# RMS norms of xa_q and ffn_up moved behind the matmul, with epilogues by half groups

## The chip, the cores and the metric

The kernel runs on one core of a Trainium2 chip. The metric is its device time in microseconds (us). Lower is better.

## The reference

One call computes two transformer blocks on 256 tokens of width 2048, batch 1. The second block ends with these steps (RMS norm, cross attention and a convolved, gated feed-forward part):

```python
def rmsnorm(x, w):
    y = xf * lax.rsqrt(jnp.mean(xf * xf, axis=-1, keepdims=True) + NORM_EPS)
    return (y * w)

h = h + merged @ w_mix_out[l]
hn = rmsnorm(h, norm_xa_w[l])
mem_n = rmsnorm(mem, norm_mem_w[l])
h = h + memory_cross_attention(hn, mem_n, xa_w_q[l], xa_w_k[l], xa_w_v[l], xa_w_o[l])
hn = rmsnorm(h, norm_ffn_w[l])
h = h + conv_gated_ffn(hn, ffn_w_up[l], ffn_conv_w[l], ffn_conv_b[l], ffn_w_down[l])
return rmsnorm(h, final_norm_w)
```

The attention has 4 heads of 512 over 256 memory tokens. The feed-forward part multiplies by a weight of 2048 x 11264, runs a causal convolution with three taps over the tokens, takes silu of one half times the other half, and multiplies by a weight of 5632 x 2048. The factor rsqrt(mean) is one number per token, and the weight is one number per feature.

## The kernel before, in words

**Data.** Activations lie with features on the 128 partitions and tokens along the row: x is 16 chunks of 128 features, each of 256 tokens. Every operand of a matmul is split into a high and a low part of type fp32r ("pair"): ScalarE copies the high part, VectorE subtracts it from the value and writes the low part. a_pair and b_pair are two such activations of 16 chunks.

**Units.** The weights stream from memory in units of 128 x 1024 (512 KB). A ring of four slots holds raw, w_hi and w_lo. For each unit SP loads raw (L572), ScalarE casts w_hi (L1154), VectorE subtracts w_lo (L1717), and PE multiplies. A unit is four chunks of the input for 256 output features. Per chunk there are two matmuls of w_hi with high and low tokens (512 columns, L688) and two of w_lo with the high tokens (256 columns, L692). The high and low products lie side by side in the accumulator.

**Stages.** `STAGES` lists the matrices in order; the four engines walk through it with loops of their own and meet through counting semaphores. In mode "F" a group of units gives two chunks of output (256 features); with 16 chunks of input a group is 4 units, and groups alternate between two halves of the accumulator. A stage of 2048 x 2048 has 32 units. ffn_up has 11 iterations of 16 units (two groups of gate features, two of value features), ffn_down has 88 units. Between stages nothing stops the stream of units: `unit_at` lets the walk of a stage split the first four units of the next one.

**The order on ScalarE and VectorE** is written out in `walk`. When unit j ends a group, they do, in this order: the join (ScalarE copies the low product to halves_b, L1185; VectorE adds it to the high product into buf_a, L1784); the split of unit j + 4; after every second group the first part of the stage's epilogue ("whole"), on four chunks; and after the split of unit j + 5 the epilogue's rest. A `side` function runs at given units j, ahead of the split. The last stage's end has no following unit, so the rest runs at once.

**Epilogues around the change.** mix_out and xa_o: VectorE adds buf_a to x (L2222), ScalarE squares (L1490), VectorE reduces the squares of four chunks to one (L2232). After the last unit PE sums over the partitions with a matrix of ones (`sums_of`, L719). Then come ScalarE's root (`rms`, L1247), VectorE's reciprocal (L1822), and `pair`: eight times two chunks of x times weight times rstd (L1849), high part (L1262), low part (L1831). `pair_ready` counts them, and the next stage's PE waits for two counts per unit. ffn_up: after two groups ScalarE does four Identities with bias and scale (L1654), VectorE eight convolution steps (L2569). For the gate half ScalarE then applies silu (L1662). For the value half VectorE multiplies with the gate (L2576), ScalarE copies the high part (L1664) and VectorE subtracts the low part of h_pair (L2581).

**Attention** runs as a side function in xa_q and xa_o: at units 9, 10 and 11 after the start of each head's eight units PE computes scores (L1052), transposes (L1061) and the product with the values (L1072). The scores wait for `dve_done`, which VectorE raises once the head's four chunks of xa_qf are written. Its keys and values (mem_k, mem_v, 2 MB each) are loaded by SP ahead of xa_q's units (L604, L605).

Of the kernel before, what the change touches and what calls it, by code (L numbers as in the profile page):

```python
# [94 lines left out]
class Stage:  # L95
    def __init__(self, name, weights, mode, iters, group_units=DC // KU, groups=2, ada=None, gate=False, act=1, dve=0, ready=0):
        self.name, self.weights, self.mode, self.iters = name, weights, mode, iters
# [116 lines left out]
for _place, _n in MOD_PLACE.items():  # L214
# [10 lines left out]
    ("rglru", 16, 36, 16), ("xa_norm", 1, 1, 0), ("xa_pair", 0, 8, 8), ("attention", 12, 12, 8),  # L225
    ("ffn_norm", 1, 1, 0), ("ffn_pair", 0, 8, 8), ("final", 1, 1, 1),
# [36 lines left out]
def rg_root_step(q):  # L263
# [5 lines left out]
            xa=68, xa_o=72, ffn=80, ffn_down=91)  # L269

# [65 lines left out]
def build(nc, t):  # L336

    ctx = ExitStack()
    with ctx:
# [14 lines left out]
        w_lo = sb("w_lo", [P, RING, KU, NCOL], F32R)  # L354
        a_pair = sb("a_pair", [P, 2, DC, T], F32R)
        a_hi, a_lo = Half(a_pair, 0), Half(a_pair, 1)
        x = sb("x", [P, DC, T])
# [60 lines left out]
        xa_qf = wk("xa_qf", [P, DC, T], 32 * K)  # L418
        xa_kf = wk("xa_kf", [P, DC, T], 48 * K)
        xa_vt = wk("xa_vt", [P, 2, D], 64 * K)  # L420
# [3 lines left out]
        h_pair = wk("h_pair", [P, 2, FC, T], 0, F32R)  # L424
# [15 lines left out]
        mean = sb("mean", [P, T])  # L440

# [61 lines left out]

        def used(stage):

            return RING + stage.u0 + stage.total
# [8 lines left out]
        def _(sp):  # L515
# [39 lines left out]
            def load(stage):  # L555
                for i in rounds(sp, stage.iters):
                    for j, (kind, g, k, _) in enumerate(stage.kinds):
# [3 lines left out]
                        if stage.name == "merge_a" and j == 2 * RING:  # L561

                            sp.wait_ge(unit_used, used(STAGE["ret_proj"]))
                            nc.sync.dma_start(rg_w[:], t["rg_w"]).then_inc(rg_in, 16)

                        sp.wait_ge(lo_done, i * stage.n + (u + 1))
                        if kind == "w":
                            src, at_ = t[stage.weights], i * stage.n_w + (g * stage.group_units + k)
                        else:
                            src, at_ = t["w_gate"], k  # L570
# [4 lines left out]
            for stage in STAGES:  # L575
# [23 lines left out]
                if stage.name == "xa_q":  # L599

                    sp.wait_ge(pair_ready, PAIR["mix_out"])
                    sp.wait_ge(kv_stored[0], 16 * 5)
                    sp.wait_ge(kv_stored[1], 16 * 5)
                    nc.sync.dma_start(flat(xa_kf), t["mem_k"]).then_inc(xa_in, 16)  # L604
                    nc.sync.dma_start(flat(xa_vt), t["mem_v"]).then_inc(xa_in, 16)  # L605
# [11 lines left out]
        def _(pe):  # L617
# [94 lines left out]
            def sums_of(stage, with_mean=False):  # L712

                for q in range(4):

                    pe.wait_ge(dve_done, DVE_DONE[stage] - 2 * (3 - q))
# [316 lines left out]
            sums_of("mix_out")  # L1033
            steps.end("xa_norm")
            steps.end("xa_pair")


# [45 lines left out]
            steps.end("ffn_norm")  # L1083
            steps.end("ffn_pair")


            run("ffn_up", a_pair, PAIR["xa_o"], batch=2)
# [54 lines left out]
        def _(act):  # L1142
# [24 lines left out]
            def run(name, group, side=None):  # L1167
# [8 lines left out]
                def finish(i, g, n_used):  # L1176
# [14 lines left out]
                    return whole if g % 2 and group else None  # L1191
# [52 lines left out]
            def rms(name):  # L1244

                steps.wait(pe=1)
                steps.done(nc.scalar.activation(spare[:], msc[:, 0, 0:T], ACT.Sqrt, bias=tiny[:, 21:22],  # L1247
# [365 lines left out]
            run("mix_out", with_squares(None))  # L1613
            rms("xa_norm")
            pair(a_hi, "xa_pair")


            def attention(first):

                def side(j):  # L1620
# [13 lines left out]
                    if step == 2:  # L1634

                        steps.wait(pe=3 * h + 3)
                        steps.done(nc.scalar.copy(b_hi[:, 4 * h:4 * h + 4, :].rearrange("p a b -> p (a b)"),
# [5 lines left out]
            run("xa_q", with_dve(None), side=attention(0))  # L1643
            run("xa_o", with_squares(None), side=attention(STAGE["xa_q"].n))
            rms("ffn_norm")
            pair(a_hi, "ffn_pair")


            def gate_and_value(i, g):
                dst = buf_b if g == 0 else buf_c  # L1650

                for m in range(4):
                    at_ = FC * g + m
# [4 lines left out]
                def rest():  # L1658

                    act.wait_ge(dve_done, dve.add())  # L1660
                    if g == 0:
                        ran(nc.scalar.activation(flat(buf_b), flat(buf_b), ACT.Silu))  # L1662
                    else:
                        ran(nc.scalar.copy(flat(h_hi)[:, bass.ds(i * (4 * T), 4 * T)], flat(buf_c)))  # L1664
                return rest

            run("ffn_up", gate_and_value)
# [37 lines left out]
        def _(dve):  # L1705
# [59 lines left out]
            def run(name, group, between=None, side=None, dest=None):  # L1765
# [4 lines left out]
                def finish(i, g, n_used):  # L1770
# [15 lines left out]
                    def whole():  # L1786
                        dve.drain()
                        return group(i, g // 2)
                    return whole if g % 2 else None
# [29 lines left out]
            def reciprocal_of_root(n):  # L1819
# [3 lines left out]
                dve.drain()  # L1823

# [694 lines left out]
            run("mix_out", residual(1.0))  # L2519
            reciprocal_of_root(1)  # L2520
            steps.end("xa_norm")
            pair(a_hi, a_lo, rms_of(x, "norm_xa"), "xa_pair")


            def attention(first):

                def side(j):
# [14 lines left out]
                    if step == 2:  # L2542

                        steps.wait(act=3 * h + 3)
                        vec.tensor_tensor(b_lo[:, 4 * h:4 * h + 4, :].rearrange("p a b -> p (a b)"),  # L2545
                                          msc[:, 2:4, :].rearrange("p a b -> p (a b)"),
                                          b_hi[:, 4 * h:4 * h + 4, :].bitcast(F32).rearrange("p a b -> p (a b)"),
# [5 lines left out]
            run("xa_q", finished, side=attention(0), dest=in_slab(xa_qf))  # L2553
            run("xa_o", residual(1.0), side=attention(STAGE["xa_q"].n))
            reciprocal_of_root(1)
            steps.end("ffn_norm")
            pair(a_hi, a_lo, rms_of(x, "norm_ffn"), "ffn_pair")


            def gate_and_value(i, g):  # L2560
                wait_act()
                dst = buf_b if g == 0 else buf_c

                for shift in (1, 2):
                    if shift == 2:
                        dve.drain()
                    for m in range(4):
                        weight = prm[:, bass.ds(i * 4 + (COL["ffn_conv_w"] + 2 * FC * (2 - shift) + FC * g + m), 1)]
                        vec.scalar_tensor_tensor(dst[:, m, shift:T], buf_a[:, m, 0:T - shift], weight,  # L2569
                                                 dst[:, m, shift:T], ALU.mult, ALU.add)  # L2570
                dve.drain()
                if g == 0:
# [3 lines left out]
                ran(vec.tensor_tensor(flat(buf_c), flat(buf_c), flat(buf_b), ALU.mult))  # L2576

                def rest():

                    wait_act()  # L2580
                    vec.tensor_tensor(flat(h_lo)[:, bass.ds(i * (4 * T), 4 * T)], flat(buf_c),  # L2581
                                      flat(h_hi)[:, bass.ds(i * (4 * T), 4 * T)].bitcast(F32),
                                      ALU.subtract).then_inc(pair_ready, 1)
                return rest

            run("ffn_up", gate_and_value)
# [152 lines left out]
```

## Time and profile before

| what | value |
|---|---|
| median of 3 runs | 3309.81 us (3309.08 to 3312.45) |
| profiled execution, its own time | 3308.2 us |
| its span, first to last instruction | 3306.4 us |
| mean granted TensorE clock | 0.973 |
| PE busy | 3120.8 us, 94% |
| PE weight loads busy | 2679.6 us, 81% |
| VectorE (DVE) busy | 2213.5 us, 67% |
| ScalarE (ACT) busy | 1626.0 us, 49% |
| GpSimd (POOL) busy | 55.6 us, 2% |
| chain that ended last | PE 84%, DVE 9%, ACT 3% |
| memory traffic | 662.04 MB, mean 200 GB/s |

The profile is one execution. Busy times of the engines overlap. In its rows L688 is line 688 of the kernel, "out<-in" are the kernel's names. PE's granted clock is given as a share of full speed, 2.4 GHz. The profiled execution's own time is its span and 1.8 us around it.

### The profile page before, as it was taken

Reading aid. Unit: us, or ns where it says so; the run is one execution under the profiler, and the core shown is the slowest. Engines: PE = TensorE matmul, PEld = TensorE weight load, DVE = VectorE, ACT = ScalarE, POOL = GpSimd, SP = SyncE. Lnnn points to the kernel's source line nnn. Section 1 sums busy time; section 2 is a strip of 40 time slices with the busy share of each in tenths; the row PEclk is TensorE's granted clock in tenths of the full one; section 3 lists DMA queues with packets and bytes.
Section 4 is the critical chain, followed back from the end, with each engine's and each line's share of the span. In section 5 each row is a group of like instructions: output and inputs, shape, how many; then the busy total and the mean of one; then the engine's idle time right before and its main releaser. Section 6 shows DMA issues by size and latency. Waiting matters only on the chain.

```text
span 3306.4 us, 45891 instructions
## 1 busy us (share of the span) xinstructions
PE 3120.8 (94%) x16880; PEld 2679.6 (81%) x16880; DVE 2213.5 (67%) x2661; ACT 1626.0 (49%) x1886; POOL 55.6 (2%) x52
## 2 busy tenths in 40 slices
PE   7999898999979997899999989998998999999997
PEld 5878787788868886688888878887887888888886
DVE  7667877668867877755665785566546667766444
ACT  5555444245544455543454665444434566655432
POOL 0000330000000000000000000000000000000000
PEclk9999999999989998899999999999999999999999
DMA  7887667377737764464455545556444555555553
GB/s 279 320 311 252 226 218 258 118 270 281 273 125 235 278 235 146 135 193 144 153 197 190 174 158 187 188 189 218 134 145 146 186 193 188 181 195 186 191 188 127
DMA packets 179516, 662.04 MB, mean 200 GB/s; under 512 B 20004, under 2 KB 20388, under 8 KB 178216
## 3 DMA queue, kind: packets, MB, share of 16 engines
q1 hardware_dynamic: 177704, 655.89, 58.7%
q10 hardware_dynamic: 1664, 4.19, 0.3%
q8 instruction: 91, 1.49, 0.2%
q14 instruction: 57, 0.47, 0.0%
HBM read 653.71 MB, written 6.29 MB: 200 GB/s over the span
## 4 chain that ended last, share of the span: by engine, by line
PE 84%; DVE 9%; ACT 3%; DVEq 2%; issue 2%; DMA 1%; ACTq 0%; SPq 0%
PE acc L688 44%; PE acc L692 22%; PE acc L699 4%; PE acc L701 4%; PE acc L700 4%; DVE w_lo L1717 2%; ACT w_hi L1154 1%; DVE gate_ratio L2472 1%; PE msc L646 1%; PE msc L648 1%; DVE mod_raw L1728 1%; DMA mod_raw<-in_w_mod 1%; PE msc L798 0%; PE acc L850 0%; PE msc L1052 0%
## 5 line engine op out<-in xcount | busy, mean ns | idle before, releaser
L1717 DVE TENSOR_TENSOR w_lo<-raw,w_hi 128x1024 fp32r<-128x1024 f32 x1020 | 1242.5, 1227 | 713.2 <-ACT w_hi L1154 704.4
L688 PE MATMUL acc<-a_pair,w_hi 128*128 128x512 f32 x4864 | 1546.8, 399 | 47.1 <-DVE w_lo L1717 16.0
L1154 ACT CAST w_hi<-raw 128x1024 fp32r<-128x1024 f32 x1020 | 1062.7, 1049 | 914.4 <-PE acc L692 679.5
L692 PEld LDWEIGHTS acc<-a_pair,w_lo 128*128 128x128 f32 x4864 | 919.8, 189 | 218.0
L692 PE MATMUL acc<-a_pair,w_lo 128*128 128x256 f32 x4864 | 960.5, 279 | 0.0
L688 PEld LDWEIGHTS acc<-a_pair,w_hi 128*128 128x128 f32 x4864 | 750.6, 190 | 56.9 <-issue 34.9
L688 PE MATMUL acc<-b_pair,w_hi 128*128 128x512 f32 x1280 | 402.3, 396 | 2.4 <-DVE b_pair L2545 2.4
L692 PEld LDWEIGHTS acc<-b_pair,w_lo 128*128 128x128 f32 x1280 | 240.4, 188 | 56.8
L699 PE MATMUL acc<-w_hi,a_pair 128*128 128x512 f32 x640 | 255.1, 399 | 27.4 <-DVE w_lo L1717 16.2
L1185 ACT COPY halves_b<-acc 128x512 f32<-128x512 f32 x200 | 117.3, 586 | 314.0 <-PE acc L692 313.9
L700 PE MATMUL acc<-w_hi,a_pair 128*128 128x512 f32 x640 | 253.4, 396 | 0.0
L701 PE MATMUL acc<-w_lo,a_pair 128*128 128x512 f32 x640 | 253.1, 396 | 0.0
L692 PE MATMUL acc<-b_pair,w_lo 128*128 128x256 f32 x1280 | 251.4, 278 | 0.0
L688 PE MATMUL acc<-h_pair,w_hi 128*128 128x512 f32 x704 | 221.2, 395 | 0.7 <-DVE w_lo L1717 0.7
L688 PEld LDWEIGHTS acc<-b_pair,w_hi 128*128 128x128 f32 x1280 | 194.9, 189 | 2.8 <-DVE b_pair L2545 2.8
L1784 DVE TENSOR_TENSOR buf_a<-acc,halves_b 128x512 f32<-128x512 f32 x160 | 110.7, 692 | 124.5 <-ACT halves_b L1185 118.5
L699 PEld LDWEIGHTS acc<-w_hi,a_pair 128*128 128x128 f32 x640 | 122.9, 192 | 55.6 <-DVE w_lo L1717 18.0
L1728 DVE SCALAR_TENSOR_TENSOR mod_raw<-mod_raw,cond_wide 128x1024 f32<-128x1024 f32 x128 | 160.0, 1250 | 10.1 <-DMA mod_raw<-in_w_mod 6.7
L692 PEld LDWEIGHTS acc<-h_pair,w_lo 128*128 128x128 f32 x704 | 132.2, 188 | 31.3
L701 PEld LDWEIGHTS acc<-w_lo,a_pair 128*128 128x128 f32 x640 | 122.7, 192 | 26.3
L700 PEld LDWEIGHTS acc<-w_hi,a_pair 128*128 128x128 f32 x640 | 122.9, 192 | 25.5
L692 PE MATMUL acc<-h_pair,w_lo 128*128 128x256 f32 x704 | 138.3, 278 | 0.0
(319 smaller groups left out, 1974.3 us busy)
## 6 DMA issues: line engine op xcount, KB each, us to landing
raw<-in_w_ffn_up SPq DMA_DIRECT2D x176, 512.0 KB, 4.2
mod_raw<-in_w_mod SPq DMA_DIRECT2D x128, 512.0 KB, 5.2
raw<-in_w_ffn_down SPq DMA_DIRECT2D x88, 512.0 KB, 3.7
ada_raw<-in_w_ada SPq DMA_DIRECT2D x64, 512.0 KB, 5.5
raw<-in_w_xa_k SPq DMA_DIRECT2D x32, 512.0 KB, 5.1
raw<-in_w_xa_v SPq DMA_DIRECT2D x32, 512.0 KB, 4.6
raw<-in_w_k SPq DMA_DIRECT2D x32, 512.0 KB, 4.3
raw<-in_w_v SPq DMA_DIRECT2D x32, 512.0 KB, 5.1
```

Of the source, the lines that this page charges most:

```text
L646: pe.matmul(msc[:, bank, :], cond_pair[:, kc, :], w_hi[:, slot, c, :], start=(first and c == 0), stop=False)
L648: mm = pe.matmul(msc[:, bank, :], cond_pair[:, kc, :], w_lo[:, slot, c, :], start=False, stop=(last and c == KU - 1))
L688: pe.matmul(acc[:, 2 * (g % 2) + m, :], w_h[:, cols], pair[:, :, kc, :], start=begin, stop=False, skip_group_check=True)
L692: mm = pe.matmul(acc[:, 2 * (g % 2) + m, 0:T], w_l[:, cols], pair[:, 0, kc, :], start=False, stop=end, skip_group_check=True)
L699: pe.matmul(out, xh, w_hi[:, slot, c, :], start=begin, stop=False)
L700: pe.matmul(out, xl, w_hi[:, slot, c, :], start=False, stop=False)
L701: mm = pe.matmul(out, xh, w_lo[:, slot, c, :], start=False, stop=end)
L1154: nc.scalar.copy(w_hi[:, slot], source).then_inc(hi_done, 1)
L1185: nc.scalar.copy(halves_b[:], low_part(g)).then_inc(part_copied, 1)
L1717: vec.tensor_tensor(w_lo[:, slot], source, w_hi[:, slot].bitcast(F32), ALU.subtract).then_inc(lo_done, 1)
L1728: vec.scalar_tensor_tensor(mod_raw[:, n % MOD_RING], mod_raw[:, n % MOD_RING], 1.0, cond_wide[:, half * (D // 2):(half + 1) * (D // 2)], A ...
L1784: vec.tensor_tensor(out, main_part(g), halves_b[:], ALU.add).then_inc(acc_free, 1)
```

## The change

- mix_out and xa_o run their epilogue after every half group (two chunks, one group of units) instead of every four chunks. VectorE adds to x. ScalarE writes the high part of x times the norm's weight (without the token factor), VectorE the low part, which raises `pair_ready`. After every second half group come square and reduce, as before. mix_out becomes one iteration of eight half groups instead of two of four.
- The token factor is computed in a side function at unit 3 (`NORM_AT`) of the following stage: PE's sums, ScalarE's root, VectorE's reciprocal. `xa_norm` and `ffn_norm` keep their steps, `xa_pair` and `ffn_pair` are gone.
- xa_q and ffn_up multiply each half group's result by the token factor on VectorE, after the split of unit j + 4.
- ffn_up is divided into ffn_first (one iteration, 16 units) and ffn_up (10 iterations), and its epilogue runs on two chunks after each group of units.
- The load of mem_k and mem_v stands at unit 10 of mix_out. Buffers are placed anew: xa_q reads b_pair, xa_o reads a_pair, ffn_up reads a new f_pair, h_pair begins where a_pair lies.

```diff
-    Stage("mix_out", "w_mix_out", "F", 2, act=1, dve=2),
+    Stage("mix_out", "w_mix_out", "F", 1, groups=4, act=3, dve=3),
     Stage("xa_q", "w_xa_q", "F", 1, groups=4, act=0, dve=1),
-    Stage("xa_o", "w_xa_o", "F", 1, groups=4, act=1, dve=2),
-    Stage("ffn_up", "w_ffn_up", "F", 11, act=2, dve=1, ready=0.5),
+    Stage("xa_o", "w_xa_o", "F", 1, groups=4, act=3, dve=3),
+    Stage("ffn_first", "w_ffn_up", "F", 1, act=4, dve=4, ready=0.5),
+    Stage("ffn_up", "w_ffn_up", "F", 10, act=4, dve=4, ready=0.5, first_unit=2 * DC // KU),
...
+NORM_AT = 3
...
+                        if stage.name == "mix_out" and j == 10:
+
+                            sp.wait_ge(dve_done, DVE_DONE["rnn_proj"])
+                            sp.wait_ge(kv_stored[0], 16 * 5)
+                            sp.wait_ge(kv_stored[1], 16 * 5)
+                            nc.sync.dma_start(flat(xa_kf), t["mem_k"]).then_inc(xa_in, 16)
+                            nc.sync.dma_start(flat(xa_vt), t["mem_v"]).then_inc(xa_in, 16)
...
-                if stage.name == "xa_q":
-
-                    sp.wait_ge(pair_ready, PAIR["mix_out"])
...
             run("mix_out", a_pair, PAIR["rnn_proj"], batch=4)
-            sums_of("mix_out")
-            steps.end("xa_norm")
-            steps.end("xa_pair")
+            def token_sums(stage, name):
+
+                def side(j):
+                    if j == NORM_AT:
+                        sums_of(stage)
+                        steps.end(name)
+                return side
...
-            run("xa_q", a_pair, PAIR["mix_out"], batch=2, side=attention(0))
-            run("xa_o", b_pair, PAIR["xa"], batch=4, side=attention(STAGE["xa_q"].n))
-            sums_of("xa_o")
...
-            run("ffn_up", a_pair, PAIR["xa_o"], batch=2)
+            run("xa_q", b_pair, PAIR["mix_out"], batch=2, side=both_sides(token_sums("mix_out", "xa_norm"), attention(0)))
+            run("xa_o", a_pair, PAIR["xa"], batch=4, side=attention(STAGE["xa_q"].n))
+            run("ffn_first", f_pair, PAIR["xa_o"], batch=2, side=token_sums("xa_o", "ffn_norm"))
+            run("ffn_up", f_pair, PAIR["ffn"])
             run("ffn_down", h_pair, PAIR["ffn"], batch=4)
...
+            def scaled_and_squares(hi, weight):
+                def group(i, g):
+                    def rest():
+                        act.wait_ge(dve_done, dve.add())
+                        for c in range(2 * g, 2 * g + 2):
+                            mm = nc.scalar.activation(hi[:, c, :], x[:, c, :], ACT.Copy, scale=col(weight, c))
+                        ran(mm)
+                        if g % 2:
+                            ran(nc.scalar.activation(both, flat(x)[:, (g - 1) * (2 * T):(g + 1) * (2 * T)], ACT.Square))
...
                     def whole():
                         dve.drain()
-                        return group(i, g // 2)
-                    return whole if g % 2 else None
+                        if scale:
+
+                            mm = vec.tensor_tensor(out, out, bcast(scale, 2), ALU.mult)
+                            if g % 2 or by_half:
+                                ran(mm)
+                        if by_half:
+                            return group(i, g)
+                        return group(i, g // 2) if g % 2 else None
+                    return whole if g % 2 or scale or by_half else None
...
+            def residual_and_low(hi, lo, weight):
+                def group(i, g):
+                    part = flat(x)[:, g * (2 * T):(g + 1) * (2 * T)]
+                    ran(vec.tensor_tensor(part, part, flat(buf_a)[:, g % 2 * (2 * T):(g % 2 + 1) * (2 * T)], ALU.add))
+                    def rest():
+                        dve.drain()
+                        wait_act()
+                        for c in range(2 * g, 2 * g + 2):
+                            mm = vec.scalar_tensor_tensor(lo[:, c, :], x[:, c, :], col(weight, c), hi[:, c, :].bitcast(F32),
+                                                          ALU.mult, ALU.subtract)
+                        mm.then_inc(pair_ready, 1)
+                        if g % 2:
+                            wait_act()
+                            ran(vec.tensor_reduce(buf_b[:, g // 2, :], buf_a[:].rearrange("p c t -> p t c"), AX, ALU.add))
...
-                    for m in range(4):
+                    for m in range(2 * half, 2 * half + 2):
...
-                ran(vec.tensor_tensor(flat(buf_c), flat(buf_c), flat(buf_b), ALU.mult))
+                ran(vec.tensor_tensor(flat(buf_c)[:, part], flat(buf_c)[:, part], flat(buf_b)[:, part], ALU.mult))
```

## Rows read from the trace of the kernel before

**Rows 1.** Windows: length, busy us (instructions) of PE, PEld, DVE, ACT, POOL, clock, DMA.

```profile
2748.40:2793.00 44.60, 44.60 (x257) 38.90 (x256) 31.04 (x38) 26.74 (x32) 0.00 (x0) 1.00 0.58 188
...
2299.15:2314.52 15.37, 2.52 (x9) 1.32 (x8) 11.04 (x15) 6.20 (x8) 0.00 (x0) 0.66 0.35 115
...
2530.21:2545.39 15.18, 2.51 (x9) 1.29 (x8) 10.77 (x14) 6.20 (x8) 0.00 (x0) 0.70 0.21 69
```

**Rows 2.** PE's waits after 2280 us: waiter, releaser, us, times, longest.

```profile
PE msc L719 <- DVE buf_b L2232: 16.7, 3, 6.3
...
PE msc L1052 <- DVEq L1814: 0.9, 4, 0.3
...
PE acc L688 <- DVE w_lo L1717: 0.7, 1, 0.7
```

**Rows 3.** Timeline, mix_out to xa_q: start, length, engine, operation, [idle before <- releaser].

```profile
2298.75 0.40 PE L692 MATMUL acc<-a_pair,w_lo 128*128 128x256 f32 x2
...
2298.99 1.46 PE L719 MATMUL msc<-buf_b,ones 128*128 128x256 f32 x6
2299.26 0.59 ACT L1185 COPY halves_b<-acc 128x512 f32<-128x512 f32 x1 [0.97 <-PE acc L692]
...
2302.23 1.23 DVE L2222 SCALAR_TENSOR_TENSOR x<-x,buf_a 128x1024 f32 x1 [0.18 <-issue]
2303.59 1.06 ACT L1490 ACTIVATE buf_a<-x 128x1024 f32 x1 [2.80 <-DVE x L2222]
...
2304.78 1.89 DVE L2232 TENSOR_REDUCE buf_b<-buf_a 128x1024 f32 x1 [1.32 <-ACT buf_a L1490]
...
2308.49 1.75 DVE L1822 RECIPROCAL rstd<-spare 128x256 f32<-128x256 f32 x1 [1.82 <-ACT spare L1247]
...
2313.73 0.68 DVE L1831 TENSOR_TENSOR a_pair<-buf_a,a_pair 128x512 fp32r<-128x512 f32 x1
...
2314.52 1.19 PE L688 MATMUL acc<-a_pair,w_hi 128*128 128x512 f32 x2 [6.57 <-issue]
```

**Rows 4.** Timeline, xa_o to ffn_up: PE's last and first matmuls.

```profile
2529.81 0.39 PE L692 MATMUL acc<-b_pair,w_lo 128*128 128x256 f32 x2
...
2545.39 1.22 PE L688 MATMUL acc<-a_pair,w_hi 128*128 128x512 f32 x2 [6.70 <-DVE a_pair L1831]
```

**Rows 5.** Timeline, the first head's scores in xa_q.

```profile
2340.19 1.22 DVE L1717 TENSOR_TENSOR w_lo<-raw,w_hi 128x1024 fp32r<-128x1024 f32 x1 [0.26 <-ACT w_hi L1154]
...
2340.97 0.39 PE L692 MATMUL acc<-a_pair,w_lo 128*128 128x256 f32 x2
...
2341.66 3.69 PE L1052 MATMUL msc<-xa_kf,xa_qf 128*128 128x256 f32 x16 [0.29 <-DVEq L1814]
```

**Rows 6.** Timeline of ACT and of DVE in one iteration of ffn_up.

```profile
2748.47 0.59 ACT L1185 COPY halves_b<-acc 128x512 f32<-128x512 f32 x1 [1.81 <-PE acc L692]
...
2749.96 2.08 ACT L1654 ACTIVATE buf_b<-buf_a,prm 128x256 f32<-128x256 f32 x4
...
2770.77 0.59 ACT L1185 COPY halves_b<-acc 128x512 f32<-128x512 f32 x1 [1.81 <-PE acc L692]
...
2774.48 1.67 DVE L2569 SCALAR_TENSOR_TENSOR buf_c<-buf_a,prm,buf_c 128x255 f32<-128x255 f32 x4 [0.91 <-ACT buf_c L1654]
...
2779.20 1.22 DVE L1717 TENSOR_TENSOR w_lo<-raw,w_hi 128x1024 fp32r<-128x1024 f32 x1
...
2782.85 2.36 DVE L1717 TENSOR_TENSOR w_lo<-raw,w_hi 128x1024 fp32r<-128x1024 f32 x2 [0.98 <-ACT w_hi L1154]
```

**Rows 7.** Timeline, start of ffn_down.

```profile
3048.72 3.49 DVE L1717 TENSOR_TENSOR w_lo<-raw,w_hi 128x1024 fp32r<-128x1024 f32 x3
...
3049.99 0.74 PE L688 MATMUL acc<-h_pair,w_hi 128*128 128x512 f32 x2 [0.67 <-DVE w_lo L1717]
```

**Rows 8.** Timeline, the first splits of xa_q behind the load of mem_k and mem_v.

```profile
2294.68 1.05 ACT L1154 CAST w_hi<-raw 128x1024 fp32r<-128x1024 f32 x1 [5.11 <-DMA raw<-in_w_xa_q]
...
2295.76 3.79 DVE L1717 TENSOR_TENSOR w_lo<-raw,w_hi 128x1024 fp32r<-128x1024 f32 x3 [4.93 <-ACT w_hi L1154]
```

More of the change, by code:

```diff
@@ L1242, in with_dve, with rms @@
                 return wrapped
-            def rms(name):
+            def rms(name, root=spare):
                 steps.wait(pe=1)
-                steps.done(nc.scalar.activation(spare[:], msc[:, 0, 0:T], ACT.Sqrt, bias=tiny[:, 21:22],
+                steps.done(nc.scalar.activation(root[:], msc[:, 0, 0:T], ACT.Sqrt, bias=tiny[:, 21:22],
                                                 scale=1.0 / D))
@@ L1641, in attention, with gate_and_value @@
                 return side
[L1643 to L1650, printed above, removed]
-                for m in range(4):
-                    at_ = FC * g + m
+            run("xa_q", with_dve(None), side=both_sides(token_root("xa_norm"), attention(0)))
+            run("xa_o", scaled_and_squares(f_hi, "norm_ffn"), side=attention(STAGE["xa_q"].n), by_half=True)
+            def gate_and_value(first, i, g):
+                half = g % 2
+                dst = buf_b if g < 2 else buf_c
+                act.wait_ge(dve_done, dve.add())
+                for m in range(2 * half, 2 * half + 2):
+                    at_ = FC * (g // 2) + 4 * first + m
                     mm = nc.scalar.activation(dst[:, m, :], buf_a[:, m, :], ACT.Identity, bias=prm[:, bass.ds(i * 4 + (COL["ffn_conv_b"] + at_), 1)],
@@ L1660, in rest @@
                     act.wait_ge(dve_done, dve.add())
[L1661 to L1662 removed]
+                    part = flat(dst)[:, half * (2 * T):(half + 1) * (2 * T)]
+                    if g < 2:
+                        ran(nc.scalar.activation(part, part, ACT.Silu))
                     else:
[L1664 removed]
+                        ran(nc.scalar.copy(flat(h_hi)[:, bass.ds(i * (4 * T) + (first * (4 * T) + half * (2 * T)), 2 * T)], part))
                 return rest
[L1667 removed]
+            run("ffn_first", lambda i, g: gate_and_value(0, i, g), side=token_root("ffn_norm"), by_half=True)
+            run("ffn_up", lambda i, g: gate_and_value(1, i, g), by_half=True)
             run("ffn_down", with_squares(None))
@@ L1763, in make_gates, with run @@
                 steps.done(vec.reciprocal(gate_tmp[64:P, 3, :], gate_tmp[64:P, 1, :]))
-            def run(name, group, between=None, side=None, dest=None):
+            def run(name, group, between=None, side=None, dest=None, scale=None, by_half=False):
                 stage = STAGE[name]
@@ L1823, in reciprocal_of_root, with token_reciprocal, side @@
                 dve.drain()
+            def token_reciprocal(name):
+                def side(j):
+                    if j == NORM_AT:
+                        steps.wait(act=1)
+                        vec.reciprocal(token_scale[:], token_scale[:])
+                        dve.drain()
+                        steps.end(name)
+                return side
             def pair(hi, lo, make, name, before=None):
@@ L2518, in _ @@
             run("rnn_proj", merge_second)
[L2519 to L2522, printed above, removed]
+            def residual_and_low(hi, lo, weight):
[3 more added lines that the diff above has]
+                    def rest():
+                        dve.drain()
+                        wait_act()
[6 more added lines that the diff above has]
+                            ran(vec.tensor_reduce(buf_b[:, g // 2, :], buf_a[:].rearrange("p c t -> p t c"), AX, ALU.add))
+                    return rest
+                return group
+            run("mix_out", residual_and_low(b_hi, b_lo, "norm_xa"), by_half=True)
             def attention(first):
@@ L2551, in attention, with gate_and_value @@
                 return side
[L2553 to L2560, printed above, removed]
+            run("xa_q", lambda i, g: None, side=both_sides(token_reciprocal("xa_norm"), attention(0)), dest=in_slab(xa_qf),
+                scale=token_scale)
+            run("xa_o", residual_and_low(f_hi, f_lo, "norm_ffn"), side=attention(STAGE["xa_q"].n), by_half=True)
+            def gate_and_value(first, i, g):
+                half = g % 2
                 wait_act()
-                dst = buf_b if g == 0 else buf_c
+                dst = buf_b if g < 2 else buf_c
                 for shift in (1, 2):
```

84 lines of the change are left out of this document (50 added, 34 removed).

## The prediction

> **What bounds the kernel now.** I read the page first: PE is busy for 3120.8 of 3306.4 us, and the chain that ended last is 84% PE. So time can only be won where PE stands still or runs slowly. Next I read the windows, stage by stage. In ffn_up PE is busy for all 44.60 us of one iteration at a granted clock of 1.00, with VectorE at 31.04 and ScalarE at 26.74 us [rows 1]. Between mix_out and xa_q, and again between xa_o and ffn_up, are stretches of 15.37 and 15.18 us with 2.5 us of PE work each and a clock of 0.66 and 0.70 [rows 1]. Third, PE's waits over the last 1000 us: besides those two places there is little, 0.9 us in four waits before the attention scores and 0.7 us at the start of ffn_down [rows 2].
>
> The timeline of the first boundary shows the ladder [rows 3]. PE's last matmul ends at 2299.15. Then follow, one after the other, a w_lo split, x (1.23 us), the square (1.06), the reduce (1.89), the last column sum, root, reciprocal and the first scaled chunks. PE starts xa_q at 2314.52. The second boundary is alike: 2530.2 to 2545.39 [rows 4].
>
> **What the two boundaries cost today.** A unit (four chunks) takes PE (2770.77 - 2748.47) / 8 = 2.7875 us at full clock [rows 6]. After the first gap nine units end at 2341.37, 26.85 us after the start instead of 25.09 [rows 3, 5]: 1.76 us, since the clock was still at 1.2 instead of 2.4 GHz for the first chunks. After the second, the group that ScalarE picks up at 2748.47 ended at 2748.36 (0.11 before, as at 2299.26 against 2299.15 [rows 3, 6]). That is 202.97 us after 2545.39, instead of 72 units or 200.70: 2.27 us. Together 15.37 + 1.76 + 15.18 + 2.27 = **34.58 us**.
>
> **The change, part by part.**
>
> *Norm moved behind the matmul.* xa_q and ffn_up now multiply the unscaled x times the norm's weight, so their first units need neither root nor reciprocal. xa_q's unit k reads the 4(k+1)-th chunk at most, and each half group of mix_out signals two chunks. Units 0 to 2 need half groups 0 to 5, which ended more than two unit lengths before. Unit 3 needs half group 7. PE can therefore go from mix_out's last unit straight into units 0 to 2, which last 8.36 us. The two other conditions hold too: accumulators alternate, and the four slots of weights ahead are filled as before.
>
> Now the last half group, counted from PE's end (0 = 2299.15) [rows 3]: the w_lo split before x is over at 2.90, x starts at 3.08 and takes 0.69 on 512 columns (like a_pair's 0.68) to 3.77; two scaled copies on ScalarE, 0.49 us apart and 0.6 long (buf_b's four take 2.08 [rows 6]), to 4.95; low halves, two of about 0.45, to 5.9; square to 6.1; reduce of 1.89 to 8.1. Unit 3's chunks are ready 2.5 us early, and the last column sum is ready 0.3 us before PE asks for it at 8.36. So the gap and the slow start both go: -34.58.
>
> *What PE now pays.* The eight matmuls of the sums stand in the stream before unit 3. Six took 1.46 us [rows 3], so eight cost 1.95, twice: **+3.9**. Root and reciprocal (the latter 1.75 us [rows 3]) must be over before VectorE scales the group that ends with unit 3, at 8.36 + 1.95 + 2.79 = 13.1. They are: sums end at 10.3, reciprocal by about 13.4 behind a w_lo, and the scale multiply comes only after another w_lo. The first weight split of the new stage that queues behind the reduce ends at about 9.3 and is due at 13.1.
>
> *Scale multiply in xa_q.* One more VectorE instruction of 128x512 after each half group, behind the w_lo. For each of the four heads PE already waits for exactly that point: w_lo ends at 2341.41, the scores start at 2341.66 [rows 5], and PE was free at 2341.37. The multiply replaces a drain and adds about 0.7 us to each head: **+2.8**. A multiply with a broadcast operand isn't in the trace; from below it is a plain one (0.68), from above two of them (1.37), which would add another 2.8. I take 0.69, as its sizes are those of the plain row.
>
> *ffn_up by half groups.* On VectorE each iteration gains four multiplies (2.76 us) and splits two operations of 1024 columns. Two of 0.685 for one of 1.23 is 0.14 more each. 31.04 + 2.76 + 0.29 = 34.1 of 44.6 us: it is covered on average. The local deadline matters more. Slots allow w_lo of the unit five further on to end four units (11.15 us) after the group's end, and the next one at 13.94. Today, from the value group's end (2770.66), they end at 9.76 and 13.4 [rows 6]: only 0.5 us to spare on the second, because four Identities, eight convolution steps, a 1024-wide product and a table load stand in one heap. New: w_lo 2.9, multiply to 3.8, two Identities to 4.95, four convolution steps of 0.42 with their drain to 7.0 (today eight in 3.5 [rows 6]), half product to 7.7, w_lo to **8.95**. ScalarE's cast of the half to 8.5, table load to 9.8, next cast, and w_lo to 12.2. Both are earlier than today, so I cost the whole edit at nothing. If the cover went, each microsecond past 11.15 would be paid in each of 44 half groups.
>
> A rule of the Trainium skill speaks against just this. *VectorE: DVE Perf Modes*, section "The TRN2 errata — SBUF-src ops pay a fixed extra latency per instruction", says that many small tiles pay a fixed latency each, and advises 512 elements or more. Its fp32 formula (N + 151) / 0.96 gives 0.69 us for 512 columns; the trace agrees (0.68 to 0.69). By it a split costs 0.157 us instead of the rows' 0.14: for 22 splits 3.5 against 3.1 us of VectorE. The sum would be 3.5 or 3.1 worse only if VectorE were the bound there.
>
> *Start of ffn_down.* PE waited 0.67 us for a w_lo that starts at 3048.72, right behind the low half of h [rows 7]. The half-wide ladder is some 3 us shorter (two Identities, four steps, and half of product, cast and low half less, the multiply more): **-0.7**. The same ladder now stands between ffn_first and the loop; by it w_lo ends some 0.6 us before its deadline.
>
> *The load of mem_k and mem_v* moves from before xa_q's units into mix_out, at unit 10. Today it holds the next cast until 2294.68, and three w_lo run to 2299.55, the first to 2297.0, before PE needs it at 2299.15 [rows 8]: 2 us to spare. The waits in front of it (rnn_proj done) are met long before; SP keeps the same order of two large transfers and then a unit. In mid-stage the same delay meets the same slack: nothing. If PE came to wait it would be 1 to 4 us, once.
>
> *Extra work in mix_out and xa_o*: per pair of half groups four scaled copies (2 us) on ScalarE, and four low halves (1.8) and 0.15 on VectorE, in 22.3 us that hold eight splits of 1.23, two joins, x and a reduce, together 14.4. Covered.
>
> Sum: -34.58 + 3.9 + 2.8 - 0.7 = **-28.6 us**. The profiled execution took 3308.2 (span 3306.4 and 1.8 around it), so 3279.6. The median shown, 3309.81, is 1.6 above that execution; carried over: **3281.3**.
>
> **Rivals.**
> A: the half-group ladder becomes the bound in ffn_up, so the kernel is slower. Place: ScalarE and VectorE hand over four times per half group, now 44 times instead of 22. For it: only 0.5 us to spare today [rows 6] and multiplies added. Against: 8.95 against 11.15. It outweighs the gain from 28.6 / 44 = 0.65 us of stall each, that is, a ladder 2.85 us longer than worked out. At 0.8 us: 35.2 - 28.6 = +6.6, 3316.4.
> B: the same ladder slips a little, at loop boundaries where the table load stands: 0.3 to 0.8 us in each of 11 iterations, 3285 to 3290.
> C: the last sum isn't ready. The margin is 0.3 us, the ladder has four handovers, and scaled copies of this form with Copy are not in the trace. 1 us late at both places: 3283. For it the small margin, against it that every duration has a near row.
> D: the burst in mix_out stalls PE: +1 to 4, 3282 to 3285.
> E: the change doesn't do what it says, PE still waits for the last pair before unit 0: the gap shrinks only by root, reciprocal and sum (about 5 us each), 3300. Against: the counts above.
>
> **Chances.** Forecast 0.77 (own range 3278 to 3285), A 0.03, B 0.08, C 0.05, D 0.04, E 0.02; another 0.01 for no change. Unknown prices reach from the attention's multiplies hidden (-2.8) to a double-priced broadcast (+2.8) and sums at 0.38 instead of 0.24 us a matmul (+2.2). The range 3277 to 3288 takes these in and most of B, C and D. About 0.2% (6.6 us) is what a measurement of this kernel can tell from no change: faster 0.95, same 0.02, slower 0.03.
>
> **What would show it.** PE's waits after 2200 us hold no entry of 6 us; the granted clock stays 1.00 across both boundaries; eight sum matmuls of about 1.95 us stand between units 2 and 3. The waits before the scores grow from 0.9 to about 3.7 us in four. In ffn_up PE is busy throughout and VectorE's share rises to about 76%. ffn_down starts without a wait. I would be wrong if PE shows waits for w_lo in ffn_up, or a wait at the sums above 0.5 us.

## The result, and the profile after

| | before | after |
|---|---|---|
| median | 3309.44 us (3308.07 to 3312.45, 4 runs) | 3283.93 us (3279.66 to 3287.07, 4 runs) |
| ratio | | 0.9922 (95% interval 0.9906 to 0.9938) |
| profiled execution, its span | 3308.2, 3306.4 us | 3283.0, 3281.2 us |
| granted clock | 0.973 | 0.976 |

The kernel is 25.5 us faster, 0.8%, where the prediction's sum was 28.6; 3283.93 lies inside the range of 3277 to 3288.

The windows of the changed kernel over both boundaries and one iteration of ffn_up (length, then busy us and instructions of PE, PEld, DVE, ACT, POOL, then granted clock, DMA share, GB/s) answer to [rows 1]:

```profile
2299.00:2330.00 31.00, 30.64 (x175) 26.60 (x173) 21.02 (x21) 15.63 (x19) 0.00 (x0) 1.00 0.55 177
...
2519.00:2545.00 26.00, 26.00 (x149) 22.69 (x148) 19.63 (x21) 16.11 (x20) 0.00 (x0) 1.00 0.49 162
...
2719.50:2764.10 44.60, 44.60 (x257) 38.90 (x256) 34.22 (x45) 24.44 (x32) 0.00 (x0) 1.00 0.56 188
```

Both gaps are gone and the clock stays at full speed across them. VectorE's share in ffn_up rose from 31.04 to 34.22 us, PE is busy throughout.

PE's waits after 2150 us (waiter, releaser, us in total, times, longest) answer to [rows 2]:

```profile
PE msc L735 <- DVE buf_b L2292: 4.5, 1, 4.5
PE msc L1072 <- DVE xa_qf L1833: 3.6, 4, 1.0
PE acc L704 <- DVE a_pair L2623: 2.4, 1, 2.4
PE acc L704 <- DVE w_lo L1760: 1.6, 1, 1.6
PE msc L1081 <- DVE prob L2618: 0.8, 4, 0.2
```

The first is the end of the kernel and was there before, as were the third and the fifth. The scores' wait grew from 0.9 to 3.6 us. The fourth is new. The wait at the start of ffn_down [rows 7] is gone.

The timeline of the first boundary, all engines (start, length, engine, operation, [idle before <- releaser]), answers to [rows 3]:

```profile
2303.36 1.05 ACT L1172 CAST w_hi<-raw 128x1024 fp32r<-128x1024 f32 x1
...
2305.76 0.69 DVE L2584 TENSOR_TENSOR x<-x,buf_a 128x512 f32<-128x512 f32 x1
...
2306.55 0.91 ACT L1641 ACTIVATE b_pair<-x,prm 128x256 fp32r<-128x256 f32 x2 [2.14 <-DVE x L2584]
...
2307.49 0.88 DVE L2591 SCALAR_TENSOR_TENSOR b_pair<-x,prm,b_pair 128x256 fp32r<-128x256 f32 x2 [1.04 <-ACT b_pair L1641]
...
2308.44 2.05 DVE L2597 TENSOR_REDUCE buf_b<-buf_a 128x256 f32<-128x1024 f32 x1
...
2311.03 1.89 PE L735 MATMUL msc<-buf_b,ones 128*128 128x256 f32 x8
```

ScalarE picked up mix_out's last group at 2302.87, so PE ended it at 2302.76 and went straight on. Until the sums it ran three units of xa_q. The reduce was over at 2310.5, 7.7 us after that end (forecast: 8.1).

**Where the time went.** ScalarE's copy of each group's low product (0.11 us after PE's last matmul of the group) is a mark in both traces:

| stretch | before | after | difference |
|---|---|---|---|
| start to the end of rnn_proj's last group but one (same code) | 2209.78 | 2211.59 | +1.8 |
| to the end of mix_out | 89.48 | 91.28 | +1.8 |
| to the end of xa_o | 230.98 | 218.42 | -12.6 |
| to ffn_down's last group | 754.14 | 737.42 | -16.7 |
| rest | 22.0 | 22.5 | +0.5 |

The first line is no work of the change: over the 12 traces of this study that mark lies anywhere from 2206.3 to 2215.6, as wide a spread as the runs of one kernel show (3279.66 to 3287.07). That it causes their spread isn't shown, as there is one trace of each kernel. Below, "the stretch" is the time from that mark to ffn_down's last group: 1074.6 us before, 1047.1 after, -27.5. It tells single microseconds apart where the medians can't.

### The profile page after: what moved, and what is told of

Same layout as the page of the kernel before. It is cut to its first block, busy times and chain, and to the rows that moved or that the text cites. A ratio compares the mean times of both kernels' runs of the same rounds, so it can differ in the third digit from the quotient of the medians.

```text
span 3281.2 us, 45848 instructions
## 1 busy us (share of the span) xinstructions
PE 3118.3 (95%) x16880; PEld 2678.6 (82%) x16880; DVE 2245.4 (68%) x2727; ACT 1610.5 (49%) x1905; POOL 55.7 (2%) x52
## 4 chain that ended last, share of the span: by engine, by line
PE 84%; DVE 9%; ACT 2%; DVEq 2%; issue 1%; DMA 1%; ACTq 0%; SPq 0%
PE acc L704 44%; PE acc L708 22%; PE acc L715 4%; PE acc L716 4%; PE acc L717 4%; DVE w_lo L1760 2%; ACT w_hi L1172 1%; DVE gate_ratio L2532 1%; PE msc L662 1%; PE msc L664 1%; DVE mod_raw L1771 1%; DMA mod_raw<-in_w_mod 1%; PE msc L814 0%; DMA raw<-in_w_mix_out 0%; PE acc L866 0%
## 5 line engine op out<-in xcount | busy, mean ns | idle before, releaser
L704 PE MATMUL acc<-a_pair,w_hi 128*128 128x512 f32 x3456 | 1102.4, 400 | 37.3 <-DVE w_lo L1760 17.2
L708 PEld LDWEIGHTS acc<-a_pair,w_lo 128*128 128x128 f32 x3456 | 654.8, 189 | 155.3
L708 PE MATMUL acc<-a_pair,w_lo 128*128 128x256 f32 x3456 | 683.7, 279 | 0.0
L704 PEld LDWEIGHTS acc<-a_pair,w_hi 128*128 128x128 f32 x3456 | 535.4, 191 | 46.0 <-issue 19.6
L704 PE MATMUL acc<-f_pair,w_hi 128*128 128x512 f32 x1408 | 442.4, 395 | 0.0
L708 PEld LDWEIGHTS acc<-f_pair,w_lo 128*128 128x128 f32 x1408 | 264.5, 188 | 62.5
L715 PE MATMUL acc<-w_hi,a_pair 128*128 128x512 f32 x640 | 255.6, 399 | 26.7 <-DVE w_lo L1760 15.5
L708 PE MATMUL acc<-f_pair,w_lo 128*128 128x256 f32 x1408 | 276.6, 278 | 0.0
L704 PEld LDWEIGHTS acc<-f_pair,w_hi 128*128 128x128 f32 x1408 | 214.4, 189 | 0.1
L715 PEld LDWEIGHTS acc<-w_hi,a_pair 128*128 128x128 f32 x640 | 123.1, 192 | 55.6 <-DVE w_lo L1760 17.7
```

The source lines that it names most:

```text
L704: pe.matmul(acc[:, 2 * (g % 2) + m, :], w_h[:, cols], pair[:, :, kc, :], start=begin, stop=False, skip_group_check=True)
L708: mm = pe.matmul(acc[:, 2 * (g % 2) + m, 0:T], w_l[:, cols], pair[:, 0, kc, :], start=False, stop=end, skip_group_check=True)
L715: pe.matmul(out, xh, w_hi[:, slot, c, :], start=begin, stop=False)
```

## The experiments

Each kernel is the changed one with one edit, unless said otherwise. They ran in three groups (e1 to e4, e5 to e8, e9 and e10), on three chips. The kernel before ran beside each group, at medians of 3310.37, 3308.41 and 3309.08 us, and each ratio is to the one of its group.

**The load of mem_k and mem_v later** (e1).

```diff
-                        if stage.name == "mix_out" and j == 10:
+                        if stage.name == "mix_out" and j == 17:
```

> The changed kernel with the load of mem_k and mem_v at unit 17 of mix_out instead of unit 10. Theory (the two large transfers meet the bunch of units that VectorE releases late behind rnn_proj's last epilogue): the one wait of PE for a w_lo in mix_out, 1.6 us, is gone, the cast behind the burst waits for its unit at most 6 us instead of 9.3, and the time falls by 1.6 us. Rival (the half-group epilogues of mix_out leave no room for a burst anywhere in the stage): PE waits 1 to 3 us at units 17 to 20 instead, and the time stays.

The place in the changed kernel first: ScalarE's wait for the unit behind the two transfers, PE's wait, and VectorE's work just before SP issued them.

```profile
2238.88 1.05 ACT L1172 CAST w_hi<-raw 128x1024 fp32r<-128x1024 f32 x1 [9.29 <-DMA raw<-in_w_mix_out]
...
2241.24 0.74 PE L704 MATMUL acc<-a_pair,w_hi 128*128 128x512 f32 x2 [1.64 <-DVE w_lo L1760]
```

```profile
2219.67 3.49 DVE L1760 TENSOR_TENSOR w_lo<-raw,w_hi 128x1024 fp32r<-128x1024 f32 x3
```

SP issued the two large transfers at 2222.50 and 2222.90 and unit 10 at 2223.38; that unit's cast began 15.5 us later, against 12.4 at the old place (2282.33 to 2294.68). mem_v took 14.7 us to land instead of 12.4. VectorE did three w_lo in a row behind rnn_proj's epilogue (2219.67 to 2223.16), and each let SP send a unit: at 2220.92, 2222.06 and 2223.38, with the two large transfers in between. In e1's trace the unit behind the transfers went out at 2239.77 and its cast began 11.8 us later. There ScalarE waited for that load 5.2 us at most:

```profile
ACT w_hi L1172 <- DMA raw<-in_w_mix_out: 5.4, 2, 5.2
```

PE has no wait for a w_lo there any more, and mix_out took 89.35 us instead of 91.28, 1.9 less. Median 3281.2 us (3278.88 to 3283.04), ratio to before 0.9913 (0.9894 to 0.9932). The wait is gone as the theory said. The whole stretch, though, fell by only 0.5 us, to 1046.6. The missing 1.4 us are in the clock, at a place where nothing was changed: the wait of 2.4 us for the last head's low part. Windows around that wait, in the changed kernel, then in e1:

```profile
2438.00:2446.00 8.00, 5.83 (x33) 5.13 (x34) 3.08 (x3) 2.39 (x3) 0.00 (x0) 1.00 0.17 60
```

```profile
2434.00:2443.00 9.00, 8.32 (x39) 7.18 (x40) 3.24 (x4) 2.45 (x3) 0.00 (x0) 0.81 0.02 5
```

The same idle time of PE (2.4 us in both) was followed by a drop to 1.2 GHz in one execution and not in the other. By the time from mix_out's end to xa_o's (219.85 instead of 218.42 in e1), five of the 12 traces have the drop, at 1.4 to 1.6 us each.

**The multiply ahead of the split** (e2).

```diff
                     vec.tensor_tensor(out, main_part(g), halves_b[:], ALU.add).then_inc(acc_free, 1)
+                    if scale:
+                        dve.drain()
+                        mm = vec.tensor_tensor(out, out, bcast(scale, 2), ALU.mult)
+                        if g % 2 or by_half:
+                            ran(mm)
 
                     def whole():
                         dve.drain()
-                        if scale:
-
-                            mm = vec.tensor_tensor(out, out, bcast(scale, 2), ALU.mult)
-                            if g % 2 or by_half:
-                                ran(mm)
```

> The changed kernel with VectorE's multiply by the token factor ahead of the split of the next weights instead of behind it (xa_q and ffn_up). Theory (the scores wait for the multiply only because a w_lo of 1.23 us stands before it): PE's four waits of 0.9 us before the scores, 3.6 us, fall to 0; the w_lo behind it ends 0.7 us later, well before PE needs it, so no new wait; time 3.6 us less. In ffn_up VectorE's wait of 1.4 us for the two Identities in each half group shrinks under 0.5 us, PE stays fully busy. Rival (the later w_lo costs what the earlier multiply gives): waits for w_lo in xa_q of 0.7 us per half group, time the same or up to 5 us more.

Median 3279.31 us (3276.33 to 3281.29), ratio 0.9904 (0.9884 to 0.9923). The waits before the scores are not in the list any more, and the time from mix_out's end to xa_o's fell by 4.7 us, to 213.8. That is 1.1 more than the 3.6 us of listed waits; why is open. The stretch is 1044.6, only 2.6 less, as mix_out took 2.1 us longer. Its stall was 2.4 instead of 1.6 us, and behind it PE ran at half the clock for a while:

```profile
2241.78 1.22 PE L704 MATMUL acc<-a_pair,w_hi 128*128 128x512 f32 x2 [2.43 <-DVE w_lo L1760]
```

The same two matmuls took 0.74 us behind the stall of the changed kernel, and the granted clock from 2238 to 2243 was 0.83 here and 1.00 there. The edit doesn't touch that stage. The theory holds for the scores. VectorE's wait for the Identities in each half group of ffn_up fell from 1.4 to 0.3 us.

**Both** (e3).

> Both edits, the late load and the early multiply. Theory: the gains add, 1.6 + 3.6 = 5.2 us less than the changed kernel, about 3278.7, and PE has no wait over 0.3 us after 2200 us but the one for the last head's low part (2.4) and the last reduce (4.5). Rival (one of them only moves the wait into the attention steps, where PE waits for prob): at most 2 us less.

Median 3275.69 us (3273.64 to 3280.38), ratio 0.9893 (0.9874 to 0.9911); the stretch is 1040.5, 6.6 less than the changed kernel's. After 2200 us PE waits only for the last head's low part (2.4), the last reduce (4.5) and prob (0.8 in four). The gains add: mix_out took 1.9 us less, as in e1, and xa_q with xa_o 4.7 less, as in e2. The median is 8.2 us below the changed kernel's, though the slowest run here (3280.38) and the fastest there (3279.66) overlap.

**The sums at unit 2** (e4).

```diff
-NORM_AT = 3
+NORM_AT = 2
```

> The changed kernel with the token factor computed at unit 2 of the next stage instead of unit 3. Theory (the last reduce ends 7.65 us after PE's last unit, and only the third unit covers it): PE reaches the sums after two units, 5.57 us, and waits 2.1 us at each boundary, 4.2 us more in all. Rival (the sums never depended closely on the reduce, the cover is ample): no wait, same time.

PE's two groups of sums at the first boundary:

```profile
2302.18 1.46 PE L735 MATMUL msc<-buf_b,ones 128*128 128x256 f32 x6
...
2304.39 0.70 PE L735 MATMUL msc<-buf_b,ones 128*128 128x256 f32 x2 [0.75 <-DVE buf_b L2597]
```

PE waits, so the reduce does come close, but 0.75 us and not 2.1: six of the eight matmuls need earlier reduces only and run for 1.46 us meanwhile. I had left them out, here and in the prediction. The group that holds the sums grew from 12.88 to 13.90 us, so the two boundaries cost 2.0 us more, half of the theory's 4.2. Median 3284.33 us (3280.31 to 3286.43), ratio 0.9923 (0.9903 to 0.9942), which can't be told from the changed kernel's.

**The second boundary alone** (e5). mix_out, its norm, `pair` (writing b_pair), xa_q and the place of the mem_k and mem_v load as before the change; everything from xa_o on as in the changed kernel.

```diff
-    Stage("mix_out", "w_mix_out", "F", 1, groups=4, act=3, dve=3),
+    Stage("mix_out", "w_mix_out", "F", 2, act=1, dve=2),
...
-            run("mix_out", residual_and_low(b_hi, b_lo, "norm_xa"), by_half=True)
+            run("mix_out", residual(1.0))
+            reciprocal_of_root(1)
+            steps.end("xa_norm")
+            pair(b_hi, b_lo, rms_of(x, "norm_xa"), "xa_pair")
...
+            run("xa_q", finished, side=attention(0), dest=in_slab(xa_qf))
```

> Only the second boundary changed: mix_out, its norm and xa_q as before (norm ahead of the matmul, load of mem_k and mem_v ahead of xa_q's units), xa_o, ffn_first, ffn_up and ffn_down as in the changed kernel. Theory (each boundary gives its own gap and slow start back, less its sums, and nothing else depends on the other): the gap between mix_out and xa_q stays at 15.4 us with a clock of 0.66, the one between xa_o and ffn_first is gone; against the kernel before 15.18 + 2.27 - 1.73 + 0.67 = 16.4 us less, about 3294. Rival (half of the gain lies elsewhere, such as the table loads or the half-wide ladder of ffn_up): more than 20 or less than 12 us less.

Median 3290.89 us (3290.72 to 3292.37), ratio 0.9945 (0.9929 to 0.9962). The stretch is 1058.1, 16.5 less than before: the 16.4 of the theory. The other boundary is still there in PE's waits:

```profile
PE msc L735 <- DVE buf_b L2297: 10.8, 2, 6.3
PE acc L704 <- issue: 6.6, 1, 6.6
```

The first boundary is then worth 1058.1 - 1047.1 = 11.0 us: 15.4 us of gap and slow start less sums, minus 2.7 for the scores and 1.6 to 1.8 for the load.

**ffn_up by whole groups** (e6), the multiply kept.

```diff
-    Stage("ffn_up", "w_ffn_up", "F", 10, act=4, dve=4, ready=0.5, first_unit=2 * DC // KU),
+    Stage("ffn_up", "w_ffn_up", "F", 10, act=2, dve=2, ready=0.5, first_unit=2 * DC // KU),
...
-                for m in range(2 * half, 2 * half + 2):
+                for m in range(4):
...
-            run("ffn_up", lambda i, g: gate_and_value(1, i, g), scale=token_scale, by_half=True)
+            run("ffn_up", lambda i, g: gate_and_value(1, i, g), scale=token_scale)
```

> The changed kernel with ffn_first's and ffn_up's epilogue on four chunks after every second group, as before the change, with the multiply by the token factor kept. Theory (the half-wide ladder is what makes room for the multiply): for the value half the w_lo of the fifth unit ends 11.75 us after the group, past the 11.15 at which PE needs it, so PE waits about 0.6 us in each of 11 iterations, and 2.5 to 3 us at the two ends (ffn_first to ffn_up, ffn_up to ffn_down), 10 to 12 us more than the changed kernel. Rival (fewer and wider instructions are cheaper on VectorE, so whole groups are at least as good): no new wait, VectorE's busy time in an iteration 0.3 us less, time the same.

Median 3303.9 us (3299.67 to 3308.44, 10 runs), ratio 0.9986 (0.9976 to 0.9995). 20.0 of the 25.5 us gained are lost. The value half's ladder on VectorE:

```profile
2711.07 0.69 DVE L1831 TENSOR_TENSOR buf_a<-buf_a,token_scale 128x512 f32<-128x512 f32 x1
2714.16 1.67 DVE L2643 SCALAR_TENSOR_TENSOR buf_c<-buf_a,prm,buf_c 128x255 f32<-128x255 f32 x4 [2.39 <-ACT buf_c L1694]
...
2717.73 1.23 DVE L2651 TENSOR_TENSOR buf_c<-buf_c,buf_b 128x1024 f32<-128x1024 f32 x1
2718.88 1.22 DVE L1758 TENSOR_TENSOR w_lo<-raw,w_hi 128x1024 fp32r<-128x1024 f32 x1
```

ScalarE picked this group up at 2708.18, so it ended at 2708.07 and w_lo at 2720.10: 12.0 us, 0.9 past the 11.15. The theory is right in kind, and its 10 to 12 us were too few: the stretch is 22.6 longer. Eight middle iterations take 46.0 us each instead of 44.6, 11.5 in all. The first takes 5.1 more, the last 1.1, and ffn_down's first group 4.7. PE waits 2.9 us once near the start of the loop and once at the start of ffn_down, and the granted clock around these waits is 0.90 (2575 to 2592) and 0.89 (3040 to 3056), so half the clock followed each of them.

**One and two more operations behind the wait** (e7, e8), and two ahead of it (e9). The added work uses values of x and an unused buffer.

```diff
                 half = g % 2
                 wait_act()
+                for k in range(2):
+                    vec.tensor_tensor(cond_wide[:, 2 * T * k:2 * T * (k + 1)], flat(x)[:, 0:2 * T], flat(x)[:, 2 * T:4 * T], ALU.max)
                 dst = buf_b if g < 2 else buf_c
```

> The changed kernel with one VectorE operation of 128x512 added to the ladder of each half group of ffn_up, right after the wait for the Identities; its result is not used. It adds 0.61 us of ladder, so VectorE is busy 36.7 of 44.6 us in an iteration. View D (a deadline: w_lo of the fifth unit at 8.9 us against 11.15): 9.5, no wait, same time. View L (VectorE's own loop in order: 11.1 us for a value and 9.9 for a gate half group with its 1.4 us wait for the Identities, 10.5 on average against 11.15): 11.1 on average, just inside, PE waits at most 0.3 us an iteration, at most 3 us more.

> The same with two such operations, 1.25 us of ladder, VectorE busy 39.2 of 44.6 us. View D (deadline): 10.15 us against 11.15, no wait, same time. View L (VectorE's loop in order): 11.75 us on average against 11.15, so PE waits 0.6 us in each of 44 half groups, 20 to 30 us more, although VectorE is busy for only 86%.

> The same two added VectorE operations of 128x512 per half group of ffn_up, but ahead of the wait for the Identities instead of behind it (results not used). View L (VectorE's loop in order, with a wait of 1.4 us in which it stands idle): the 1.3 us fill that wait, the loop stays at 10.5 us on average, PE has no new wait, time within 2 us of the changed kernel, though VectorE is busy for the same 39 of 44.6 us as with two behind the wait. Rival (VectorE's work itself is the bound at 86 to 88%): as slow as with two behind the wait, 20 to 25 us more.

Measured: 3283.01 us with one more (3281.67 to 3286.13, ratio 0.9919, 0.9902 to 0.9935); 3308.71 with two (3302.02 to 3316.21, 10 runs, ratio 0.9997, 0.9987 to 1.0007); 3282.89 with two ahead of the wait (3280.84 to 3285.69, ratio 0.9915, 0.9899 to 0.9932). View D falls, view L holds. With one more, only the loop's first iteration is longer, by 0.5 us. With two more, a middle iteration takes 46.69 us instead of 44.59, 2.1 more where view L had 2.4. VectorE with two more, one half group:

```profile
2711.21 0.69 DVE L1827 TENSOR_TENSOR buf_a<-acc,halves_b 128x512 f32<-128x512 f32 x1 [0.17 <-issue]
2711.82 1.22 DVE L1760 TENSOR_TENSOR w_lo<-raw,w_hi 128x1024 fp32r<-128x1024 f32 x1
2713.12 0.69 DVE L1833 TENSOR_TENSOR buf_a<-buf_a,token_scale 128x512 f32<-128x512 f32 x1
2715.11 1.29 DVE L2640 TENSOR_TENSOR cond_wide<-x 128x512 f32<-128x512 f32 x2 [1.29 <-ACT buf_c L1695]
...
2723.28 0.69 DVE L1827 TENSOR_TENSOR buf_a<-acc,halves_b 128x512 f32<-128x512 f32 x1 [0.18 <-issue]
```

From one join to the next are 12.07 us, against 11.15 that PE needs, and the only idle time of note in them is the 1.29 in which VectorE stands at the Identities. A gate half group takes 11.27. The windows of one iteration in e9 show the same added work at no cost:

```profile
2719.50:2764.10 44.60, 44.60 (x257) 38.91 (x257) 39.06 (x53) 24.40 (x33) 0.00 (x0) 1.00 0.56 191
```

VectorE is busy for 39.06 of 44.60 us and PE never waits. With two behind the wait it is busy for no more, 38.66 us, but in an iteration of 46.69.

**Both edits and two more** (e10).

> Both edits (late load, multiply ahead of the split) and two added VectorE operations behind the wait for the Identities. View L: with the multiply first, the wait for the Identities is 0.3 instead of 1.4 us, so VectorE's loop has 1.1 us more room per half group: 11.0 us for a value and 9.8 for a gate half group with the two more, under 11.15. PE has no new wait and the time is that of the version with both edits, about 3276 to 3279. Rival (the order of the multiply makes no difference to the room): PE waits as with two more in the changed kernel, 25 us more.

Median 3274.71 us (3272.78 to 3275.52), ratio 0.9889 (0.9873 to 0.9906). With the multiply first, what cost 25 us now costs nothing. This is no better version than e3, only e3 with idle work added; their medians can't be told apart.

## Why the prediction was right

Step by step, with the prediction's own terms (its sum comes to 3281.2 rather than 3281.3):

- *Both gaps and slow starts go, -34.6.* Right. PE doesn't stop, the clock stays 1.00, and e5 separates the second boundary at the forecast size (16.5 against 16.4). The first follows by difference only.
- *Sums, +3.9.* Measured +3.5: the group that holds them takes 12.88 instead of 11.15 us, 1.73 at each place.
- *Scores, +2.8.* Measured +2.7 (0.9 to 3.6). The multiply with a broadcast operand takes 0.69 us, the lower bound. e2 shows the place: with the multiply ahead of the w_lo the wait is gone.
- *Start of ffn_down, -0.7.* Right, the wait is gone.
- *ffn_up at nothing.* Right in time, partly by luck. The ladder came out as worked out:

```profile
2739.81 0.88 DVE L2646 SCALAR_TENSOR_TENSOR buf_c<-buf_a,prm,buf_c 128x255 f32<-128x255 f32 x2 [1.41 <-ACT buf_c L1695]
...
2741.80 0.69 DVE L2655 TENSOR_TENSOR buf_c<-buf_c,buf_b 128x512 f32<-128x512 f32 x1
2742.41 1.22 DVE L1760 TENSOR_TENSOR w_lo<-raw,w_hi 128x1024 fp32r<-128x1024 f32 x1
```

  The group ended at 2734.70, w_lo at 2743.63: 8.93 us against 8.95. The next w_lo ended at about 10.7, against 12.2 forecast with a table load in front of it that isn't there any more. But I measured the room by such deadlines, 2.2 us. The true room is VectorE's loop: four w_lo, join, multiply, steps and a wait for ScalarE in fixed order. It takes 10.4 us of 11.15, an estimate from e8 (46.69 / 4 = 11.67, less 1.3). e8 used the room up with 1.3 us more and lost 25 us. So rival A's stalls begin between 0.65 us of added ladder (e7) and 1.3, and at 1.3 they eat the whole gain. The prediction had 2.2 and 2.85. Its chance of 0.03 rested on a margin that wasn't there, and I had not seen how near the edit came to it.
- *The load of mem_k and mem_v at nothing.* Wrong: PE waited 1.6 us, and mix_out took 1.8 longer. The slip is "the same delay meets the same slack": the two transfers now start while SP sends the loads that rnn_proj's epilogue had held back, and the first unit behind them took 3.1 us longer than at the old place. e1 shows that the place does it; that the loads sent at the same time are the reason fits the 11.8 us in e1, but was not tried apart from the place. Rival D, which had the place and the size (1 to 4 us), came true beside the forecast.
- *The last sum 0.3 us early.* The margin was 2.1 us: it is the last two matmuls that need the last reduce, after 8.36 + 1.46 us, and the reduce ended at 7.7 (e4). Rival C was weighed by the wrong margin too.

The terms come to -34.6 + 3.5 + 2.7 - 0.7 + 1.6 = -27.5, which is the stretch. So the forecast of -28.6 was 1.1 us off by its terms: 1.6 for the load, less 0.4 for the sums and 0.1 for the scores. The profiled execution gained only 25.2, since 1.8 us were lost ahead of the change and 0.5 behind it, in code that is the same. The median shows 25.5.

The Trainium skill's page *VectorE: DVE Perf Modes*, section "The TRN2 errata — SBUF-src ops pay a fixed extra latency per instruction", puts a fixed latency on every VectorE instruction that reads SBUF, the on-chip memory, and the trace agrees (two halves of 0.69 us for one of 1.23). Its advice of 512 elements or more is met by the halves too, so it doesn't speak against them as the prediction has it. The wider form does take less of VectorE, 33.4 us an iteration in e6 against 34.2, and is 20 us slower all the same: the order of hand-overs decides here, not the fixed part.

## What to carry to other kernels

Where an engine works through a fixed order with waits in it, take its loop time, waits included, as its load. Here 83% busy was full (e8, 368 us of a stretch of 445 in ffn_up) and 88% was free (e9), according to which side of a wait the work stood on. A norm whose token factor commutes with the matmul can be moved behind it, and its sums then need to stand only where the last reduce has ended. Where another engine waits for the multiply's result, put the multiply ahead of the long weight split (e2). Before moving a large transfer, ask what the queue carries at the new moment (e1).

## What the runs showed that I had not expected

The same PE wait of 2.4 us was followed by half the clock in five of 12 traces, at 1.4 to 1.6 us, and by full clock in the others; e2's stall in mix_out is a further case. So a wait can cost a second time, through the clock. ffn_up also lost its table loads. From 2520 to 3200 us the kernel before has these in its loop:

```profile
L1154 ACT ACT_TABLE_LOAD x10 | 12.8, 1283 | 0.2
L1662 ACT ACT_TABLE_LOAD x10 | 12.8, 1283 | 0.2
```

The changed kernel's ACT has these in all in the same window:

```profile
L1266 ACT ACT_TABLE_LOAD x1 | 1.3, 1283 | 0.0
...
L1704 ACT ACT_TABLE_LOAD x1 | 1.3, 1283 | 0.0
```

ffn_first runs silu once ahead of the loop. That this is what lets the loop keep its table was not tried alone. The half groups are not what does it, since e6 runs whole groups and has no table load in the loop either; and so the missing table loads are not what makes room for the multiply, since e6 stalls without them.
